# Opening a two-layer decoder trunk from a transposed copy of x, with the row norms' squares summed on VectorE and TensorE

## The reference

```
y = x * rsqrt(mean(x*x, axis=-1) + 1e-6) * gain          # RMSNorm
x = x + 0.5 * (silu(y @ w_gate) * (y @ w_up)) @ w_down   # w_gate, w_up: 1024 x 2816, w_down: 2816 x 1024
```

## Time and profile before

| | |
|---|---|
| median of three runs | 1138.39 us |
| the profiled execution | 1138.71 us |
| its span in the profile | 1136.9 us |
| TensorE (PE) busy | 1133.1 us, 100% |
| VectorE (DVE) busy | 770.4 us, 68% |
| ScalarE (ACT) busy | 630.6 us, 55% |
| cold chunk on TensorE | from 8.13 us, the next chunk follows |
| first down product | begins at 32.98 us |

### The profile page before, as it was taken

The page is one execution under the profiler, slowest core; times in us unless marked ns, Lnnn a source line. Parts: engine busy times, 40 slices in busy tenths (PEclk is TensorE's granted clock), DMA queues, the critical chain, the costliest instruction groups (busy, mean ns, idle before and its releaser), DMA issues.

```text
span 1136.9 us, 16092 instructions
## 1 busy us (share of the span) xinstructions
PE 1133.1 (100%) x5975; PEld 966.9 (85%) x5975; DVE 770.4 (68%) x1055; ACT 630.6 (55%) x941; POOL 70.3 (6%) x79
## 2 busy tenths in 40 slices
PE   9999999999999999999999999999999999999999
PEld 7888888888888888888888888888887888888887
DVE  5766666868768676655766856678676695766655
ACT  6644445666674564544564544466766745544542
POOL 3020000202000000000020200002110000000000
PEclk9999999999999999999999999999999999999999
DMA  9956654545544666656566555636445445656521
GB/s 324 319 175 198 187 192 140 185 136 198 148 148 152 219 223 187 193 177 219 172 169 228 185 185 186 200 98 220 148 163 172 182 154 183 222 185 202 193 86 37
DMA packets 138828, 207.34 MB, mean 182 GB/s; under 512 B 6898, under 2 KB 99876, under 8 KB 138756
## 3 DMA queue, kind: packets, MB, share of 16 engines
q1 hardware_dynamic: 137364, 205.02, 55.1%
q0 software_dynamic: 752, 0.79, 0.8%
q10 hardware_dynamic: 640, 0.55, 0.2%
HBM read 205.29 MB, written 1.05 MB: 181 GB/s over the span
## 4 chain that ended last, share of the span: by engine, by line
PE 100%; DVE 0%; issue 0%; POOL 0%; DVEq 0%; POOLq 0%
PE bank L560 28%; PE bank L530 17%; PE bank L534 17%; PE bank L533 17%; PE bank L564 15%; PE bank L546 1%; PE bank L859 1%; PE bank L849 1%; PE bank L830 1%; PE bank L668 1%; PE bank L848 1%; PE bank L877 1%; PE bank L569 0%; PE bank L738 0%; PE bank L735 0%; PE bank L732 0%
## 5 line engine op out<-in xcount | busy, mean ns | idle before, releaser
L1300 DVE TENSOR_TENSOR w_low<-raw,w_high 128x1024 fp32r<-128x1024 f32 x388 | 464.2, 1232 | 281.4 <-ACT w_high L1016 280.8
L1016 ACT ACTIVATE w_high<-raw 128x1024 fp32r<-128x1024 f32 x387 | 393.5, 1055 | 317.8 <-PE bank L564 173.5
L560 PE MATMUL bank<-xT,w_high 128*128 128x512 f32 x1388 | 331.6, 390 | 0.1
L560 PEld LDWEIGHTS bank<-xT,w_high 128*128 128x128 f32 x1388 | 257.0, 188 | 51.2 <-DVE xT L1318 0.2
L564 PEld LDWEIGHTS bank<-xT,w_low 128*128 128x128 f32 x1408 | 175.7, 191 | 3.6
L564 PE MATMUL bank<-xT,w_low 128*128 128x256 f32 x1408 | 178.6, 283 | 0.0
L530 PE MATMUL bank<-w_high,xT 128*128 128x512 f32 (+1 forms) x440 | 171.3, 389 | 0.0
L534 PE MATMUL bank<-w_low,xT 128*128 128x512 f32 (+1 forms) x440 | 168.2, 382 | 0.0
L533 PE MATMUL bank<-w_high,xT 128*128 128x512 f32 (+1 forms) x440 | 168.1, 382 | 0.0
L530 PE MATMUL bank<-w_high,oT_high 128*128 128x512 f32 x418 | 162.6, 389 | 0.0
L534 PE MATMUL bank<-w_low,oT_high 128*128 128x512 f32 x418 | 162.2, 388 | 0.0
(11 more groups left out here) (146 smaller groups left out, 771.5 us busy)
## 6 DMA issues: line engine op xcount, KB each, us to landing
raw<-in_w_in SPq DMA_DIRECT2D x92, 512.0 KB, 4.6
raw<-in_ffn_w_down SPq DMA_DIRECT2D x88, 512.0 KB, 4.3
raw<-in_ffn_w_gate SPq DMA_DIRECT2D x86, 512.0 KB, 4.1
raw<-in_ffn_w_up SPq DMA_DIRECT2D x86, 512.0 KB, 5.0
raw<-in_w_out SPq DMA_DIRECT2D x16, 512.0 KB, 4.4
raw<-in_w_branch_c SPq DMA_DIRECT2D x8, 512.0 KB, 4.0
raw<-in_w_branch_a SPq DMA_DIRECT2D x4, 512.0 KB, 4.1
raw<-in_w_branch_b SPq DMA_DIRECT2D x4, 512.0 KB, 6.0
```

Source lines behind the costliest of these rows:

```text
L560: return nc.tensor.matmul(bank[b0 + n][:, :], w_high[:, slot, column(k, n)], xT[:, k], start=k == 0, stop=full_last and k == KB - 1)
L1016: act.activation(w_high[:, slot], raw[:, in_slot, (p % 2) * 1024:(p % 2) * 1024 + 1024], ACT.Copy).then_inc(sem["high_ready"], 1)
L1300: dve.tensor_tensor(w_low[:, slot], raw[:, FILL_SLOT[p // 2], (p % 2) * 1024:(p % 2) * 1024 + 1024], w_high[:, slot].bitcast(F32), ALU.sub ...
```

## The change

The host passes two new arrays: `x_turned`, x transposed (1024 x 256), and `gains`, all gains already as columns (128 x 2 x 26). The first `cold_first_chunk` in the diff below is ScalarE's, the second VectorE's. The kernel loads `x_turned` in five pieces of 1, 1, 2, 2 and 2 blocks into `o_nat`, which is free until the mixers. The transposes of the opening and of the gains go away. ScalarE and VectorE split x^T from SBUF. The first weight pair is loaded in two halves (128 KB of gate and of up for each block), and VectorE makes the high part of its first half (a cast) and its low part. TensorE works in smaller steps on blocks 0 and 1. `warm` runs 11 matmuls of ones in one piece.

For the norm ScalarE squares x^T (two activations of 1024 elements), VectorE adds the eight blocks with one reduce that reads with a stride, and TensorE sums over partitions with two matmuls of one column. The row is turned one wide pair and one narrow pair later than before. x itself, needed for the residual, is loaded by GpSimd's queue after the fourth chunk's hidden values; the rotary table and parameters wait for the second's.

```diff
+X_BLOCKS = ((0, 1), (1, 1), (2, 2), (4, 2), (6, 2))
+WARM = 11
...
+            load_x_turned(0)
+            load_x_turned(1)
+            first_rows(sp, 1, 1, half_landed[1], (1,))
+            load_x_turned(2)
+            first_rows(sp, 2, 2, fill_landed[FILL_SLOT[0]])
+            load_x_turned(3)
+            first_rows(sp, 4, 2, third_landed)
+            load_x_turned(4)
+            first_rows(sp, 6, 2, fill_landed[FILL_SLOT[1]])
...
-            def cold_row():
+            def sum_squares():
 
                 pe.wait_ge(sem["up_summed"], 1)
-                turn_row(0, 1, 4)
-                pe.wait_ge(rows_loaded, 16 * 3)
-                nc.tensor.transpose(bank[5][:, 0:GAIN_ROWS], gain_rows[0:GAIN_ROWS, :], ident[0:GAIN_ROWS, 0:GAIN_ROWS]).then_inc(gains_turned, 1)
+                pe.wait_ge(block_squares_summed, 1)
+                for half in range(HALVES):
+                    last = nc.tensor.matmul(bank[4][:, half:half + 1], block_sums[:, half * P:half * P + P], ones[:, 0:1].bitcast(F32),
+                                            start=True, stop=True)
+                last.then_inc(squares_summed, 1)
...
                     if opens and not turned:
-                        cold_row()
+                        sum_squares()
                     gate_up_wide(layer, p + 2, 2, done + 1, i * 12)
                     gate_up_narrow(layer, p, 0, done + 1, i * 12).then_inc(sem["pair_used"], 1)
+                    if opens and not turned:
+                        turn_row(0, 1, 4)
...
+                for first in (0, D):
+                    last = act.activation(x_squares[:, first:first + D], x_turned[:, first:first + D], ACT.Square)
+                last.then_inc(block_squares_ready, 1)
                 high(0, 4)
...
             def cold_first_chunk():
                 p = 4
                 high(0, p + 1)
                 copy_rest(0, 1)
                 high(0, p + 2)
+                high(0, p + 3)
+                act.wait_ge(squares_summed, 1)
+                act.activation(norm_sq, bank[4][:, 0:HALVES], ACT.Copy).then_inc(sem["squares_ready"], 1)
                 copy_row(0, 1)
-                high(0, p + 3)
                 silu_gate(0, 1)
                 high(0, p + 4)
-                cold_rest_gains()
                 high(0, p + 5)
                 hidden_high(0, 1, 0)
...
             def cold_first_chunk():
+                dve.wait_ge(block_squares_ready, 1)
+                dve.tensor_reduce(block_sums, x_squares.rearrange("p (k s) -> p s k", k=KB), axis=AXIS_X, op=ALU.add).then_inc(block_squares_summed, 1)
                 low(0, p)
                 low(0, p + 1)
                 sum_gate(0, 1)
                 sum_up(0, 1)
                 low(0, p + 2)
+                low(0, p + 3)
                 dve.wait_ge(sem["row_ready"], 1)
```

More of the change, by code:

```diff
@@ L220, in build, with first_rows @@
         block = ctx.enter_context(nc.Block())
[L222 to L226, removed]
+        def first_rows(engine, k0, nk, landed, parts=(0, 1)):
+            v = raw[:, FILL_SLOT[k0 // 4]].rearrange("p (k g c) -> p k g c", k=4, g=2)[:, k0 % 4:k0 % 4 + nk]
+            for g in parts:
+                w = (a["ffn1_w_gate"], a["ffn1_w_up"])[g]
+                engine.dma_start(v[:, :, g], w[0:1, k0 * P:(k0 + nk) * P, 0:FC].rearrange("o (k p) c -> p (o k) c", p=P)
                                  ).then_inc(landed, 16)
@@ L347, in ffn, with load_x_turned @@
                 fill(layer, n + FFN_PAIRS // 2 - 1, down(wd, layer, CHUNKS - 1))
[L349 to L358, removed]
-            first_rows(sp, 2, first_landed[2])
-            first_rows(sp, 3, fill_landed[FILL_SLOT[1]])
-            sp.dma_start(gain_rows[48:50, :], a["diff_subln"]).then_inc(rows_loaded, 16)
+            def load_x_turned(piece):
+                k0, nk = X_BLOCKS[piece]
+                sp.dma_start(x_turned[:, k0 * S:(k0 + nk) * S].rearrange("p (k s) -> p k s", k=nk),
+                             a["x_turned"][k0 * P:(k0 + nk) * P, :].rearrange("(k p) s -> p k s", p=P)).then_inc(x_turned_landed[piece], 16)
+            load_x_turned(0)
[7 more added lines that the diff above has]
+            first_rows(sp, 6, 2, fill_landed[FILL_SLOT[1]])
             for layer in range(DEPTH):
@@ L667, in warm @@
                 for _ in range(count):
[L668 to L669 removed]
+                    nc.tensor.matmul(bank[7][:, :].rearrange("p (a b) -> p a b", a=4), ones[:, :],
+                                     ones[:, :].unsqueeze(1).to_broadcast([P, 4, P]), start=True, stop=True)
             def cold_chunk():
                 b0 = inner_bank(1)
[L675 to L680 removed]
                 full, high_part, low_part = inner_parts(PAIR_SLOT[0], b0)
[L682 removed]
+                pe.wait_ge(block0_high, 1)
                 pe.wait_ge(half_high, 1)
@@ L685, in cold_chunk @@
                     high_part(0, n, w_high, True)
+                pe.wait_ge(half_low, 1)
+                for n in range(4):
+                    high_part(0, n)
+                pe.wait_ge(block0_low, 1)
+                for n in range(4):
+                    low_part(0, n)
+                pe.wait_ge(sem["blocks_high"], 1)
                 pe.wait_ge(sem["high_ready"], value("high_ready", 0, 1))
@@ L1680, in rotary_constants, with gain_columns @@
     return np.ascontiguousarray(table.reshape(2, HALVES, P, DH).transpose(2, 0, 1, 3).astype(np.float32))
+def gain_columns(inputs):
+    columns = [inputs[name].reshape(DEPTH, KB, P).transpose(2, 0, 1) for name in ("ffn1_norm", "mix_norm", "ffn2_norm")]
+    columns.append(inputs["diff_subln"].reshape(DEPTH, 1, P).transpose(2, 0, 1))
+    columns.append(np.broadcast_to(np.asarray(LAM_INIT, np.float32).reshape(1, DEPTH, 1), (P, DEPTH, 1)))
+    return np.ascontiguousarray(np.concatenate(columns, axis=2).astype(np.float32))
 def kernel(**inputs):
```

164 lines of the change are left out of this document (84 added, 80 removed).

## The result

The changed kernel takes 1140.64 us (median of 22 runs, 1139.01 to 1142.8), the kernel before 1138.38 in the 22 runs beside it (1137.58 to 1138.78). The ratio is 1.0018, interval 1.0013 to 1.0024: 2.3 us slower, where 1.7 faster was forecast, and above the end of the range, 1138.9. The 22 runs fall in two groups. Ten have a mean granted clock of 1.0 and take 1139.01 to 1139.9, median 1139.2. Twelve have 0.998 or 0.999 and take 1140.56 to 1142.8, median 1141.0. Every run of before has 1.0. The profiled execution (1139.01) is the best of the first group, so the trace shows the better half of the result only; no trace of the changed kernel, here or in its repeat, is of an execution with a lower clock.

What follows compares the result with a forecast made beforehand. TensorE bounds the kernel, busy 1133.1 of 1136.9 us. The first down product at 31.3 instead of 32.98 gains 1.7 us: 1138.71 becomes 1137.0, less 0.3 for the median, 1136.7; range 1136.0 to 1137.5, chance 0.50.

Steps and rivals of the forecast that it cites:

- the opening: Kernel start to cold chunk's end: first useful product at 6.0 us, pair 1 at 9.55, end at 17.9, 3.3 us earlier.
- the last link: Before the first down product: hidden_low comes 5.9 us behind the norm's row, TensorE has 4.7 us of work, waits 1.2.
- That last sum: From the norm's row to hidden_low: 2.87 + 3.03 = 5.9 us.
- Rival A: Opening's 3.3 us stay, no late sums or hidden chain: down product at 29.6, gain 3.4 us, 1135.0; chance 0.28.
- Rival B: Opening starves: TensorE at low clock until 9.55, cold chunk ends at 19.0, gain 1.1 us; chance 0.13.
- Its second half: In the opening, pair 1's weights also land 1 us late: gain 0.1 us, 1138.3.
- the reduce: VectorE's sum of 2048 squares behind the cold chunk: 2.4 us, ending at 18.4, if a strided read costs nothing.
- rival C: Strided reduce at half speed takes 4.9 us: down product at 33.7, 0.7 us slower, 1139.1; chance 0.09.
- point of decision: The length of VectorE's reduce from which the strided-read rival decides: 4.1 us.
- the one-column matmuls: TensorE's two matmuls for the norm behind the wait for the sums: 0.3 us.
- the wide pair behind them: TensorE's wide pair between the one-column matmuls and the norm's row: 1.84 us.
- low parts and sums: VectorE behind the reduce: low parts of pairs 4 and 5 2.35 us, two sums 1.28, done at 22.1; TensorE waits 0.5.

Runs made afterwards that it cites:

- its repeat: The changed kernel run again with no edit: 1140.45 us, ratio 1.0017.
- the early pairs: The changed kernel with the high and low parts of pairs 8 and 9 made ahead of the norm's row on ScalarE and VectorE: 1140.51 us.
- hidden first: The changed kernel with hidden_high and hidden_low made ahead of pair 9's parts on ScalarE and VectorE: 1139.65 us.
- before with 512 KB more: The kernel before with an unused 512 KB load ahead of pair 1's weights: 1139.09 us.
- adds with 512 KB more: The changed kernel with three contiguous adds for the reduce, plus an unused 512 KB load ahead of pair 1's weights: 1140.31 us.
- the best version: The changed kernel with three contiguous adds for the reduce and pairs 8 and 9's parts made ahead of the norm's row: 1137.1 us.

## Why the prediction was wrong, step by step

Right were the opening and the last link. First useful product 5.81 us (6.0 forecast), pair 1 at 9.40 (9.55), the next chunk at 17.84 (cold chunk's end 17.9), ScalarE's squares 2.00 (2.03), a stall for `hidden_low` of 1.18 (1.2). That last sum writes 2.87 us where its rows give 2.83, and takes the low part of pair 8 as following on the high part, where before's rows have 0.31 us between them; the measured chain from the row to `hidden_low` is 5.8 us, so it held. Rival A fails by these stalls. Rival B (a low clock until 9.55) occurs in neither trace of the changed kernel. Its second half, pair 1's weights up to 1 us later, occurs in traces of variants with the same opening (high part of pair 1 at 8.20 us in the changed kernel, at up to 9.36). The granted clock can't rule B out for the other executions: the table gives 1.00 from the first us on, though the eleven matmuls of ones take 4.51 us, 0.41 each, against 0.23 later.

**The step that failed first is the reduce**: "The reduce of 2048 elements: one of 1024 takes 1.21 us, so 2.43 if a strided read costs nothing; [...] I take 2.4". It is 3.93, 1.92 ns an element against 1.12 in order. The contiguous reduce, the three adds, the doubled reduce and the reduce put into before show it from four sides. It was rival C, at four fifths of its size, and its point of decision (4.1 us) held to about 0.1: with 3.93 the down product came 0.05 us earlier than before. That is partly luck, since the other terms up to there missed by 0.4 us one way and by 0.5 the other. The error was the weight: 0.09, on the argument that the same count and operation take the same time. No row had such a stride, and that should have left the two ends more even.

The Trainium skill ("SBUF — State Buffer", section "Door 1: The DMA port swizzle") says that a read from SBUF is at full rate only if it hits each 16-byte line at least twice, which for fp32 limits how far one may stride. The inner axis here steps over 1 KB, so no two elements in a row share a line; 1.92 against 1.12 ns agrees. The Trainium skill ("VectorE: DVE Perf Modes", section "Mode 1× (REGULAR) — the baseline") says that odd strides all work in the fallback mode, to which it gives one result per cycle, and names no price for them. Read as the same rate for every stride, it does not agree with the measurement.

**The second term was missing: what stalls do to TensorE's clock.** I forecast 0.5 and 1.2 us of idle time and priced them as just that. The stall for the sums came out at 1.48, and the mean granted clock is below 1.0 in 18 of 33 executions. None of the 18 has a trace, so that their clock fell to 0.50 (1.2 GHz) behind that stall is concluded from other runs: the low clock is in the trace of the early pairs some 1.1 us behind the same stall, and in that of the doubled reduce from the stall's end on; filling the stalls takes it away in 11 of 11 runs; the adds, which take away only the first stall, do so too in 11 of 11. Sorted by the stalls of each version's trace, the runs below clock 1.0 are:

| stalls of TensorE, near 22 and 32 us if nothing else is said | runs below clock 1.0 |
|---|---|
| none, 0.5, or 0.8 (the stalls filled; adds with early pairs; before with one reduce more) | 0 of 33 |
| 1.2, or 1.0 and 1.2 (adds; contiguous reduce) | 0 of 22 |
| 1.48 and 1.18 (changed kernel, both sets of runs) | 18 of 33 |
| 1.48, then 0.61 at 39 us (hidden first) | 2 of 11 |
| 1.48 and 0.4 (pairs before row) | 10 of 11 |
| 5.3 and 1.1 (reduce twice) | 4 of 4 |
| 1.5 near 12 us (before with 512 KB more) | 0 of 11 |
| 2.0 near 11 us, 1.2 (adds with 512 KB more) | 3 of 11 |
| 1.86 near 13 us and four of 0.2 to 1.0 ahead of it (GpSimd squares) | 10 of 11 |

So the length of the longest stall isn't all: the early pairs and the version with the hidden values first have the same 1.48, and fall in 10 and in 2 of 11 runs, and a wait of 2.0 us goes with fewer low runs than one of 1.48. What else decides stays open.

The Trainium skill ("TensorE: Matmul & The Clock Gate", Part 1) says that the chip watches activity in windows which run free of the program. That fits a stall that drops the clock in one execution and not in the next; no run here shows a window.

**The sum, with what was measured.** From 1136.7:

- the down product begins at 32.76 instead of 31.3: 1.46. The reduce is 1.50 of it (3.93 against 2.43), the one-column matmuls 0.3 (0.61 in the chain, where I said 0.3), and the wide pair behind them 0.1 (1.97 in the chain against 1.84). Less 0.5: the squares end 0.3 earlier, and low parts and sums take 3.5 us, not 3.7;
- before stands at 32.81 by its record, where I took the chain's 32.98: 0.2;
- behind the down product, from record to record: before takes 1101.07 us from there to its last matmul, the changed kernel 1101.39, so 0.3. The forecast put this at nothing ("Behind that point the two programs run the same work"). The first down product after its stall is 0.1 of it. The other 0.2 arise in the chunk behind it: from its first wide to its first narrow matmul it takes 5.65 us against 5.44, and there a weight load waits for the chunk's second sum, which VectorE ends at 39.23 us, 0.9 into the chunk; before ended its own at 37.78, ahead of the chunk:

```profile
39.29 4.43 PEld L572 LDWEIGHTS bank<-xT,w_high 128*128 128x128 f32 x20 [0.31 <-DVE work L1380]
```

  Every variant of the changed kernel has this wait (0.3, or 0.56 with the hidden values first), none of the three traces of before and its variants does. In the changed kernel VectorE makes `hidden_low` until 32.7 us and four low parts behind it, before until 31.25;
- these make 1138.7; with the 0.3 that I took off for the median of before it is 1139.0, the profiled execution. The median of the runs at clock 1.0 is 0.2 above. I put that down to weights that land later (0.24 us later moved the repeat's end by 0.3); two traces are too few to show it;
- from 1139.2 to the median of all runs, 1140.64: 1.4, which is the low clock in more than half of them. Filling the stalls gave back 1.0 in the median. The adds gave 2.3: 1.2 against the repeat's five runs at clock 1.0 (median 1139.39), and 1.1 since none of theirs is below.

So of the 3.9 us between forecast and result, the reduce is about 1.5, the clock 1.4, and the rest are small terms.

**Where the opening's 3.2 us went.** The critical path moved off TensorE. Every step between the landing of the cold chunk's last weights and the down product is now in one row: 12.7 to 32.8 us. Before, TensorE found all of that ready when it came. The 512 KB tell the two apart: a landing 1.5 us later costs the new chain 1.6 at the down product, one 2.4 us later costs before 0.5. In the best version the chain is TensorE's again from 9.65 us on, but for the way of the norm's factor over ScalarE and GpSimd from 22.6 to 25.9. What makes the weights land up to 1.2 us later in one execution than in another (last high part of the cold chunk at 12.70 to 13.88 us in the traces) stays open.

## What to carry to other kernels

When work is taken off the busiest engine at the head of a program, follow the new chain to the first point where both programs do the same and every engine is as far ahead as it was, and price each stall on TensorE at two values, with and without the low clock behind it; 1.5 us of idle time here cost 1.6 more in the one trace that caught it. Sum over blocks with contiguous adds instead of a reduce whose inner axis strides: 2.5 us by halving adds against 3.9 for 2048 elements. An operation of a kind no row shows deserves even weights between its bounds, above all where the point of decision lies between them.

## What the runs showed of the hardware

- VectorE's fp32 reduce of 2048 elements: 3.93 us with an inner step of 1 KB, 2.29 in order.
- ScalarE's square of 1024 elements: 1.0 us writing in order, 2.1 writing with a step of 32 bytes.
- Operations of VectorE with two SBUF sources beside GpSimd's with two: 2.70 us instead of 0.87 for two of 256 elements, 2.31 instead of 1.23 for one of 1024. The Trainium skill ("SBUF — State Buffer", section "Who interferes with whom") says that such a pair contends and that the second one to issue is blocked until the first is done; the trace agrees: the low part is issued at 13.81 us, GpSimd's add of 512 elements runs from 13.75 to 15.03, and the low part takes 1.1 us more.
- The norm's factor on GpSimd (128 x 2 elements) took 0.19 and 0.71 us before, 1.19 and 0.73 in the changed kernel, where the first ends as VectorE's low parts do, and 1.19 and 1.52 beside VectorE's low parts in the best version.
- A plain f32 matmul of one column is two records, and two such matmuls take TensorE 0.47 us from start to the next.
- A stall of 1.48 us on TensorE can be enough for the clock of 1.2 GHz behind it; in the five versions of which no stall is longer than 1.2 us, none of 55 runs shows it. In the one trace that shows it the low stretch lasts from about 25.2 to 28.7 us.
